# Norms by halves of a row on two engines, transposes between products, and the last rows split over two engines

## Chip, core and metric

The kernel runs on one core of a Trainium2 chip. The metric is the device time in microseconds of one execution; lower is better. All inputs start in HBM, and the output ends there. The engines are TensorE (PE), VectorE (DVE), ScalarE (ACT), GpSimd (POOL) and SyncE (SP), each with its own queue of instructions that runs in order; semaphores tie them together.

## What is computed

A decoder trunk of two layers over 256 rows of 1024 columns in float32: latent attention, a dense SwiGLU mixer, then sliding-window attention and a mixture of 8 experts with 2 chosen for each row, and a last norm. Before each part stands the same norm:

```python
def rmsnorm(x, g):
    xf = x.astype(jnp.float32)
    y = xf * lax.rsqrt(jnp.mean(xf * xf, axis=-1, keepdims=True) + EPS)
    return (y * g.astype(jnp.float32)).astype(x.dtype)
...
    for l in range(DEPTH):
        xn = rmsnorm(h, g_attn[l])
        if l < N_A_LAYERS:
            h = h + mla(xn, ...)
        else:
            if b == 0:
                k_band, v_band, pos_band = shared_band_kv(h, positions, kv_g, kv_w, kv_b)
            h = h + swa_sink(xn, ...)
        xn = rmsnorm(h, g_ffn[l])
        h = h + (swiglu(xn, ...) if l % 2 == 0 else moe(xn, ...))
    return rmsnorm(h, g_final)
```

## The kernel before

The residual rows stay in SBUF as `h`, two tiles of 128 rows (t = 0, 1) by 1024 columns. Everything is written out by hand: each engine has one program, and the order of the instructions in it is the order of the code.

The program runs through these stages: latent attention (to about 116 us), the dense mixer (to about 321 us), keys, values and queries of the second attention and that attention (to about 410 us), routing, then a loop over the experts (from about 425 to 1243 us), and the last norm. The mixer's products use weights split in a high and a low part: ScalarE casts (`w_hi_part`, L800), VectorE subtracts (`w_lo_part`, L1754), unit by unit; TensorE multiplies high by high and low (L1140, L1141) and low by high (L1144). A unit is half of the k range of one chunk of gate or up weights. Units 0 and 1 are run for t = 0 and then for t = 1 before the others start.

Weights come through one area, `ring`, by DMAs that SyncE issues. The dense ones (L620) wait until the weights that lie there have been used. The experts' pieces (896 KB, L658; the down weights in pairs, L661) wait in `room_for` until their place is free: for the first expert until the dense weights above it are used, the last of them by the product with `swo`; afterwards until TensorE has read a piece that lies there.

A norm of a row tile is a chain over four engines. ScalarE squares 1024 columns and sums them (`squares`, L746; L968 at the end). VectorE turns the sum into mean plus EPS (L1599), GpSimd raises it to the power -0.5 (L697), VectorE scales the row (L1606, or L1608 with the gain at the end). Then TensorE transposes the scaled row in eight blocks (`rows_to_T`, L982), and VectorE takes the blocks out of PSUM with the gain: `evac_xT` (L1621) in two halves of four blocks, or, before the dense mixer, `evac_xT_split`, which writes the gained halves (L1762), lets ScalarE cast them to `xT_hi` (L809) and subtracts to get `xT_lo` (L1767). `add_out` (L1746), `ffn_add` (L1823) and `add_rows` (L1990) add a product, 512 columns at a time, to `h`. At the end of the dense mixer the four additions are split by the first tile's norm: two before it, two behind it. There the scaled rows are transposed once and taken out twice, to `xT2` with the gain of keys and values and to `xT` with the gain of the attention. `L1243` makes keys, `L1247` and `L1248` values, `L1264` queries (`sq_products`).

GpSimd has little else in its queue: some small loads, the bias `swa_b_o` added to `h` (L725), two copies of prefetched pieces (L738), and the powers. The final gain `g_final` lies in `gfin`, a row repeated over the partitions, loaded long before it is used. At the end the two tiles are scaled by VectorE and stored by two DMAs that ScalarE issues (L973); SyncE waits for both.

## Time and profile before

| what | us |
|---|---|
| median of 3 runs | 1260.67 |
| lowest, highest | 1260.46, 1261.53 |
| the profiled execution | 1258.74 |
| its span, first to last instruction | 1256.1 |
| mean granted TensorE clock, share of full | 0.996 |

In the profiled execution TensorE is busy for 1203.2 us, VectorE for 315.7, ScalarE for 256.1 and GpSimd for 30.2. 413 MB are moved by DMA. Matmuls are pipelined and their busy time is modelled, so the rows that matter are those with an engine's idle time (in square brackets, with what ended it) and the DMA share of a stretch.

### The profile page before, as it was taken

How to read it: one execution, taken by the hardware profiler on the slowest of the kernel's cores; microseconds unless marked ns; L12 is line 12 of the kernel's file. 1: busy time of each engine (PE TensorE's matmuls, PEld its weight loads, DVE VectorE, ACT ScalarE, POOL GpSimd, SP SyncE). 2: the span in 40 equal slices, each digit the busy share in tenths (PEclk: the TensorE clock that was granted, in tenths of full speed). 3: DMA queues.
4: the chain of work that ended last, by engine and by line, in shares of the span. 5: the costliest groups of instructions: out<-in, count | busy, mean ns of one | idle time of the engine just before them, and what ended most of it. 6: DMA issues, size and time to landing. Idle time of an engine off the chain costs nothing.

```text
span 1256.1 us, 20334 instructions
## 1 busy us (share of the span) xinstructions
PE 1203.2 (96%) x8373; PEld 610.5 (49%) x8374; DVE 315.7 (25%) x716; ACT 256.1 (20%) x470; POOL 30.2 (2%) x48
## 2 busy tenths in 40 slices
PE   6999999999899999898999999999999999999997
PEld 4765777778665534333333433433343343334333
DVE  2355566667353400100010010010001101000102
ACT  2252433333154111011010101102101210211111
POOL 2100000000101100000000000000000000000000
PEclk9999999999999999999999999999999999999999
DMA  9612644326622699999999999999999999999994
GB/s 339 226 68 97 239 165 171 134 103 236 257 77 101 248 423 423 419 420 428 420 419 424 421 419 422 425 419 419 425 419 417 425 422 419 422 425 410 411 427 176
DMA packets 73021, 413.17 MB, mean 329 GB/s; under 512 B 6591, under 2 KB 11837, under 8 KB 64493
## 3 DMA queue, kind: packets, MB, share of 16 engines
q1 hardware_dynamic: 71708, 409.65, 80.5%
q8 instruction: 65, 1.06, 0.3%
q0 software_dynamic: 944, 1.29, 0.3%
q10 hardware_dynamic: 288, 1.05, 0.2%
q14 instruction: 16, 0.12, 0.0%
HBM read 410.91 MB, written 1.05 MB: 328 GB/s over the span
## 4 chain that ended last, share of the span: by engine, by line
PE 81%; DMA 9%; DVE 4%; issue 2%; ACT 2%; SPq 1%; POOL 0%; DVEq 0%; ACTq 0%; POOLq 0%
PE ps L1468 17%; PE ps L1448 11%; PE ps L1443 6%; PE ps L1426 6%; DMA ring<-in_moe_w_up 5%; PE ps L1535 4%; DMA ring<-in_moe_w_down 4%; PE ps L1144 4%; PE ps L1140 4%; PE ps L1141 4%; PE ps L1430 3%; PE ps L1499 3%; PE ps L1313 2%; PE ps L1106 2%; PE ps L1519 2%
## 5 line engine op out<-in xcount | busy, mean ns | idle before, releaser
L1468 PE MATMUL ps<-ring,arena 128*64 128x448 f32 x640 | 251.1, 545 | 9.2 <-issue 4.3
L1469 PE MATMUL ps<-ring,arena 128*64 128x448 f32 x640 | 251.2, 545 | 0.0
L1448 PE MATMUL ps<-ring,arena 128*32 128x448 f32 x1152 | 161.4, 539 | 0.0
L1468 PEld LDWEIGHTS ps<-ring,arena 128*64 128x64 f32 x640 | 84.5, 137 | 156.3 <-issue 142.4
L1449 PE MATMUL ps<-ring,arena 128*32 128x448 f32 x384 | 160.0, 539 | 0.0
L2007 DVE TENSOR_TENSOR arena<-arena,ps 64x448 f32<-64x448 f32 (+1 forms) x64 | 38.5, 613 | 369.2 <-ACT arena L910 190.7
L1535 PE MATMUL ps<-ring,arena 128*64 128x512 f32 x280 | 125.1, 596 | 5.0 <-DMA ring<-in_moe_w_down 5.0
L1536 PE MATMUL ps<-ring,arena 128*64 128x512 f32 x280 | 125.1, 596 | 0.0
L1443 PE MATMUL ps<-ring,arena 128*32 128x448 f32 x768 | 90.4, 542 | 5.8 <-DVE arena L2007 4.0
L1448 PEld LDWEIGHTS ps<-ring,arena 128*32 128x32 f32 x1152 | 48.0, 110 | 93.8 <-issue 93.8
L1754 DVE TENSOR_TENSOR w_lo<-ring,w_hi 128x2048 fp32r<-128x2048 f32 x33 | 75.5, 2292 | 60.3 <-ACT w_hi L800 59.2
L1426 PE MATMUL ps<-ring,arena 128*32 128x512 f32 x504 | 87.1, 593 | 0.0
L800 ACT CAST w_hi<-ring 128x2048 fp32r<-128x2048 f32 x33 | 62.9, 1908 | 114.2 <-PE ps L1144 114.2
L1427 PE MATMUL ps<-ring,arena 128*32 128x512 f32 x168 | 86.0, 593 | 0.0
L1469 PEld LDWEIGHTS ps<-ring,arena 128*64 128x64 f32 x640 | 84.5, 137 | 0.0
L1535 PEld LDWEIGHTS ps<-ring,arena 128*64 128x64 f32 x280 | 36.7, 137 | 78.9 <-issue 73.4
L1140 PE MATMUL ps<-w_hi,xT_hi 128*128 128x512 f32 (+1 forms) x192 | 71.6, 380 | 2.8 <-DVE xT_lo L1767 2.8
L1141 PE MATMUL ps<-w_hi,xT_lo 128*128 128x512 f32 (+1 forms) x192 | 70.1, 372 | 0.0
L921 ACT COPY arena<-ps 128x320 f32<-128x320 f32 (+3 forms) x48 | 21.8, 455 | 211.5 <-PE ps L1519 211.5
L1430 PE MATMUL ps<-ring,arena 128*32 128x256 f32 x672 | 51.6, 379 | 0.0
L1990 DVE TENSOR_TENSOR h<-h,ps 128x512 f32<-128x512 f32 x36 | 24.7, 687 | 104.4 <-PE ps L1499 104.4
L1443 PEld LDWEIGHTS ps<-ring,arena 128*32 128x32 f32 x768 | 22.4, 109 | 52.3 <-issue 43.2
(292 smaller groups left out, 1421.6 us busy)
## 6 DMA issues: line engine op xcount, KB each, us to landing
ring<-in_moe_w_down SPq DMA_DIRECT2D x64, 1792.0 KB, 21.1
ring<-in_moe_w_gate SPq DMA_DIRECT2D x127, 896.0 KB, 19.4
...
```

What stands on the lines that cost most here:

```text
L1140: pe.matmul(out, lhs[0][:, k, c], rhs_hi[:, k, :], start=(first and k == 0), stop=False)
L1141: pe.matmul(out, lhs[1][:, k, c], rhs_hi[:, k, :], start=False, stop=False)
L1426: pe.matmul(ps[32 * j:32 * j + 32, bank, :], thirds[j], left, start=first, stop=last)
L1427: pe.matmul(ps[SLOTS:P, bank, :], thirds[2], right, start=first, stop=last)
L1430: mm = pe.matmul(ps[q:q + 32, bank + 1, 0:LASTQ], thirds[j], right[:, cols:cols + LASTQ], start=first, stop=last)
L1443: pe.matmul(ps[q:q + 32, 4 + c // 2, 0:CH], thirds[j], wg[:, (c + e) * CH:(c + e + 1) * CH], start=first, stop=last)
L1448: pe.matmul(ps[32 * j:32 * j + 32, c, 0:CH], thirds[j], wu[:, c * CH:(c + 1) * CH], start=first, stop=last)
L1449: mm = pe.matmul(ps[SLOTS:P, c, 0:CH], thirds[2], wg[:, c * CH:(c + 1) * CH], start=first, stop=last)
L1468: pe.matmul(ps[0:NARROW, c, 0:CH], lhs, wu[:, cols], start=(k == 0), stop=(k == KD - 1))
L1469: mm = pe.matmul(ps[64:64 + NARROW, c, 0:CH], lhs, wg[:, cols], start=(k == 0), stop=(k == KD - 1))
L1535: pe.matmul(ps[0:NARROW, DOWN_BANK, :], lhs, w[:, 0:512], start=first, stop=last)
L1536: mm = pe.matmul(ps[64:64 + NARROW, DOWN_BANK + 1, :], lhs, w[:, 512:1024], start=first, stop=last)
```

## The change

Seven semaphores are added. The two early norms (n = 1 before the dense mixer, n = 2 behind it) and the last one are done in another way; the first norm of the program and the one before the experts stay.

Squares: ScalarE squares the two 512-wide halves of a tile in instructions of their own, each as soon as its addition is done, with the factor 1/32 inside, so that the sums add up to the mean (`square_half`). GpSimd adds EPS to the lower half's sum (`rstd_of_halves`), and ScalarE adds the upper half's sum to that by an Identity activation of one column (`mean_of_halves`), in place of VectorE's instruction. GpSimd's power stays. Scaling: VectorE scales the lower half (`scale_lower`), ScalarE the upper (`scale_upper`); TensorE waits for the upper only ahead of the fifth transposed block.

Order: before the dense mixer the transposes of t = 1 go between unit 0 and unit 1 of t = 0, and each unit of t = 1 waits for its own half of the transposed rows. Behind the mixer VectorE does three additions before the scaling, and takes out `xT2` of both tiles before `xT` of either; the transposes of t = 1 go between keys and values of t = 0, and the key products wait by halves.

End: the last additions signal `h_final`. Row tile 0 is scaled by VectorE as before and stored by SyncE. Of row tile 1, GpSimd multiplies the upper half by the gain, between row 0's power and row 1's EPS addition, and ScalarE scales it and stores it; VectorE does the lower half, SyncE stores it.

TensorE's order before, around the transposes of t = 1 ahead of the dense mixer. The two groups of four L1144 rows of t = 0 end unit 0 and unit 1; this is the second:

```order
L1144 MATMUL ps<-w_lo,xT_hi 128x512 x4
L982 MATMUL ps<-cst,xn 128x128 [waits xn_ready]
L982 MATMUL ps<-cst,xn 128x128 x7
L1140 MATMUL ps<-w_hi,xT_hi 128x512 [waits xT_ready]
L1141 MATMUL ps<-w_hi,xT_lo 128x512
```

and now, where the L1193 row (the former L1144) is the first of the two:

```order
L1193 MATMUL ps<-w_lo,xT_hi 128x512 x4
L1031 MATMUL ps<-cst,xn 128x128 [waits xn_ready]
L1031 MATMUL ps<-cst,xn 128x128 x3
L1031 MATMUL ps<-cst,xn 128x128 [waits xn_ready_a]
L1031 MATMUL ps<-cst,xn 128x128 x3
L1189 MATMUL ps<-w_hi,xT_hi 128x512
```

The eight transposes moved ahead by one unit, and have a second wait in their middle.

VectorE's order before, at the end of the dense mixer (L1823 `ffn_add`, L1621 `evac_xT`, twice for each tile):

```order
L1823 TENSOR_TENSOR h<-h,ps 128x512 [waits fh_added,fdown_mm] x2
L1599 TENSOR_SCALAR stat<-stat 128x1 [waits ssq_ready]
L1606 TENSOR_SCALAR xn<-h,stat 128x1024 [waits rstd_ready]
L1823 TENSOR_TENSOR h<-h,ps 128x512 [waits fh_added,fdown_mm] x2
L1621 TENSOR_TENSOR xT<-ps,vecT 128x4x128 [waits xT_mm]
L1621 TENSOR_TENSOR xT<-ps,vecT 128x4x128
L1621 TENSOR_TENSOR xT<-ps,vecT 128x4x128 [waits xT_mm]
L1621 TENSOR_TENSOR xT<-ps,vecT 128x4x128
L1599 TENSOR_SCALAR stat<-stat 128x1 [waits ssq_ready]
L1606 TENSOR_SCALAR xn<-h,stat 128x1024 [waits rstd_ready]
L1621 TENSOR_TENSOR xT<-ps,vecT 128x4x128 [waits xT_mm]
L1621 TENSOR_TENSOR xT<-ps,vecT 128x4x128
```

and now (L1882 `ffn_add`, L1668 `scale_lower`, L1680 `evac_xT`):

```order
L1882 TENSOR_TENSOR h<-h,ps 128x512 [waits fh_added,fdown_mm] x3
L1668 TENSOR_SCALAR xn<-h,stat 128x512 [waits rstd_ready]
L1882 TENSOR_TENSOR h<-h,ps 128x512 [waits fh_added,fdown_mm]
L1680 TENSOR_TENSOR xT<-ps,vecT 128x4x128 [waits xT_mm]
L1680 TENSOR_TENSOR xT<-ps,vecT 128x4x128
L1668 TENSOR_SCALAR xn<-h,stat 128x512 [waits rstd_ready]
L1680 TENSOR_TENSOR xT<-ps,vecT 128x4x128 [waits xT_mm]
L1680 TENSOR_TENSOR xT<-ps,vecT 128x4x128
L1680 TENSOR_TENSOR xT<-ps,vecT 128x4x128 [waits xT_mm]
L1680 TENSOR_TENSOR xT<-ps,vecT 128x4x128
L1680 TENSOR_TENSOR xT<-ps,vecT 128x4x128 [waits xT_mm]
L1680 TENSOR_TENSOR xT<-ps,vecT 128x4x128
```

The third addition stands ahead of the scaling, the second tile's scaling and its `xT2` ahead of the first tile's `xT`, and the mean is gone.

GpSimd's order at the end of the program, before (L733 loads the final gain, L738 copies a prefetched piece):

```order
L697 TENSOR_TENSOR stat<-stat,cst 128x1 [waits ms_ready] x2
L733 DMA xT<-in_g_final 128x1024 [waits swo_mm]
L738 COPY ring<-arena 128x1792 [waits gu_read,ahead_loaded]
L738 COPY ring<-arena 128x1792
L697 TENSOR_TENSOR stat<-stat,cst 128x1 [waits ms_ready] x2
```

and now (L758 the copy, L718 EPS, L709 power, L762 the gain):

```order
L758 COPY ring<-arena 128x1792 [waits gu_read,ahead_loaded]
L758 COPY ring<-arena 128x1792
L718 TENSOR_SCALAR stat<-stat 128x1 [waits half_squares]
L709 TENSOR_TENSOR stat<-stat,cst 128x1 [waits ms_ready]
L762 TENSOR_TENSOR xn<-h,xT 128x512 [waits h_final,rel_loaded]
L718 TENSOR_SCALAR stat<-stat 128x1 [waits half_squares]
L709 TENSOR_TENSOR stat<-stat,cst 128x1 [waits ms_ready]
```

The EPS addition and the power of tile 1 come behind a 512-wide product.

The diff, with the declarations of semaphores cut to those that the text names:

```diff
@@ -155,7 +155,14 @@
...
+        self.half_squares = sem("half_squares")
+        self.eps_added = sem("eps_added")
+        self.xn_ready_a = sem("xn_ready_a")
+        self.h_final = sem("h_final")
...
@@ -674,7 +681,12 @@
                     sp.nop()
-            sp.wait_ge(s.out_stored, 32)
+            rows = out[0].rearrange("(t p) d -> t p d", p=P)
+            sp.wait_ge(s.row_done, 1)
+            sp.dma_start(rows[0], xn[:, 0, :]).then_inc(s.out_stored, 16)
+            sp.wait_ge(s.row_done, 2)
+            sp.dma_start(rows[1][:, 0:512], xn[:, 1, 0:512]).then_inc(s.out_stored, 16)
+            sp.wait_ge(s.out_stored, 48)
@@ -700,6 +712,12 @@
+            def rstd_of_halves(n, t):
+                pool.wait_ge(s.half_squares, 4 * n + 2 * t + 1)
+                nc.gpsimd.tensor_scalar(stat[:, 10 + t:11 + t], stat[:, 6 + t:7 + t], EPS, None, ALU.add).then_inc(s.eps_added, 1)
+                rstd(4 + t, 2 + t)
             pool.wait_ge(s.consts_loaded, 16)
@@ -714,13 +732,15 @@
                 pool.dma_start(tabs_h[32 * kk + 1:32 * kk + 32, 1, c], rel_bias[0:31, :]).then_inc(s.rel_loaded, 16)
-            rstd_rows()
-            rstd_rows()
+            for n in range(2):
+                for t in range(TT):
+                    rstd_of_halves(n, t)
...
             pool.wait_ge(s.xn_ready, 6)
+            pool.wait_ge(s.xn_ready_a, 4)
             for t in range(TT):
@@ -736,7 +756,11 @@
                 nc.gpsimd.tensor_copy(piece(m), ahead[:, n, :]).then_inc(s.piece_landed[m % LAPS], 16)
-            rstd_rows()
+            rstd_of_halves(2, 0)
+            pool.wait_ge(s.rel_loaded, 16 * 10)
+            pool.wait_ge(s.h_final, 4)
+            nc.gpsimd.tensor_tensor(xn[:, 1, 512:D], h[:, 1, 512:D], gfin[:, 512:D], ALU.mult).then_inc(s.gained_last, 1)
+            rstd_of_halves(2, 1)
@@ -744,6 +768,23 @@
                 act.activation(xn[:, t, :], h[:, t, :], ACT.Square, accum_out=stat[:, t:t + 1]).then_inc(s.ssq_ready, 1)
+            def square_half(t, half, done, count, junk):
+                act.wait_ge(done, count)
+                act.activation(junk, h[:, t, half * 512:(half + 1) * 512], ACT.Square, scale=D ** -0.5,
+                               accum_out=stat[:, 6 + 2 * half + t:7 + 2 * half + t]).then_inc(s.half_squares, 1)
+            def mean_of_halves(n, t):
+                act.wait_ge(s.half_squares, 4 * n + 2 * t + 2)
+                act.wait_ge(s.eps_added, 2 * n + t + 1)
+                act.activation(stat[:, 2 + t:3 + t], stat[:, 8 + t:9 + t], ACT.Identity, bias=stat[:, 10 + t:11 + t]).then_inc(s.ms_ready, 1)
+            def scale_upper(n, t):
+                act.wait_ge(s.rstd_ready, 5 + 2 * n + t)
+                act.activation(xn[:, t, 512:D], h[:, t, 512:D], ACT.Copy, scale=stat[:, 4 + t:5 + t]).then_inc(s.xn_ready_a, 1)
@@ -802,8 +843,10 @@
             for t in range(TT):
-                act.wait_ge(s.h_attn0, 2 * t + 2)
-                squares(t)
+                for half in range(2):
+                    square_half(t, half, s.h_attn0, 2 * t + half + 1, xn[:, t, half * 512:(half + 1) * 512])
+                mean_of_halves(0, t)
+                scale_upper(0, t)
                 for b in range(2):
@@ -825,8 +868,10 @@
             for t in range(TT):
-                act.wait_ge(s.fh_added, 4 * FCH - 2 * (TT - 1 - t))
-                squares(t)
+                for half in range(2):
+                    square_half(t, half, s.fh_added, 4 * (FCH - 1) + 2 * t + half + 1, xn[:, t, half * 512:(half + 1) * 512])
+                mean_of_halves(1, t)
+                scale_upper(1, t)
             act.wait_ge(s.kT_mm, 2)
@@ -964,13 +1009,15 @@
             for t in range(TT):
-                act.wait_ge(s.h_added, items * 4 + (2 * t + 3))
-                act.activation(xT[:].rearrange("p k n -> p (k n)")[:, t * D:(t + 1) * D], h[:, t, :], ACT.Square,
-                               accum_out=stat[:, t:t + 1]).then_inc(s.ssq_ready, 1)
+                for half in range(2):
+                    square_half(t, half, s.h_final, 2 * t + half + 1, xT[:].rearrange("p k n -> p (k n)")[:, half * 512:(half + 1) * 512])
+                mean_of_halves(2, t)
             orow = out[0].rearrange("(t p) d -> t p d", p=P)
-            for t in range(TT):
-                act.wait_ge(s.xn_ready, 9 + t)
-                act.dma_start(orow[t], xn[:, t, :]).then_inc(s.out_stored, 16)
+            act.wait_ge(s.gained_last, 1)
+            act.wait_ge(s.rstd_ready, 12)
+            act.activation(xn[:, 1, 512:D], xn[:, 1, 512:D], ACT.Copy, scale=stat[:, 5:6]).then_inc(s.row_done_a, 1)
+            act.wait_ge(s.row_done_a, 1)
+            act.dma_start(orow[1][:, 512:D], xn[:, 1, 512:D]).then_inc(s.out_stored, 16)
@@ -979,6 +1026,8 @@
                 for k in range(KD):
+                    if k == 4 and n >= 1:
+                        pe.wait_ge(s.xn_ready_a, 2 * (n - 1) + t + 1)
                     mm = pe.transpose(ps[:, off + 2 * t + k // 4, (k % 4) * P:(k % 4 + 1) * P], xn[:, t, k * P:(k + 1) * P], ident)
@@ -1215,10 +1264,11 @@
             for t in range(TT):
-                if t == 1:
-                    rows_to_T(1, 1, 4)
-                    pe.wait_ge(s.xT_ready, 8)
                 for q in range(2):
+                    if (t, q) == (0, 1):
+                        rows_to_T(1, 1, 4)
+                    if t == 1:
+                        pe.wait_ge(s.xT_ready, 7 + q)
                     p_ = gu_passes(q, t)
@@ -1236,12 +1286,13 @@
             for t in range(TT):
-                if t == 1:
-                    rows_to_T(2, 1, 0)
-                pe.wait_ge(s.xT_ready, 10 + 4 * t)
                 for k in range(KD):
+                    if k % 4 == 0:
+                        pe.wait_ge(s.xT_ready, 9 + 2 * t + k // 4)
                     mm = pe.matmul(ps[:, 4, t * P:(t + 1) * P], w[:, k, 0:P], xT2[:, k, t * P:(t + 1) * P], start=(k == 0), stop=(k == KD - 1))
                 mm.then_inc(s.kT_mm, 1)
+                if t == 0:
+                    rows_to_T(2, 1, 0)
                 b = 7 if t == 0 else 5
@@ -1486,7 +1537,7 @@
-            def scatter(i, t):
+            def scatter(i, t, last=False):
@@ -1494,7 +1545,9 @@
                     j = 2 * t + half
-                    if t == 1:
+                    if t == 1 and last:
+                        pe.wait_ge(s.h_final, half + 1)
+                    elif t == 1:
                         pe.wait_ge(s.h_added, i * 4 + (half + 2))
@@ -1575,8 +1628,8 @@
                     pe_item(i, False)
-            scatter(items, 0)
-            scatter(items, 1)
+            scatter(items, 0, True)
+            scatter(items, 1, True)
@@ -1607,6 +1660,12 @@
                                              op0=ALU.mult, op1=ALU.mult).then_inc(s.xn_ready, 1)
+            def scale_lower(t):
+                norms[0] += 1
+                dve.wait_ge(s.rstd_ready, norms[0])
+                dve.tensor_scalar(xn[:, t, 0:512], h[:, t, 0:512], stat[:, 4 + t:5 + t], None, ALU.mult).then_inc(s.xn_ready, 1)
@@ -1771,11 +1830,11 @@
             add_out(1, s.wo_mm, s.h_attn0)
-            norm_rows(0)
+            scale_lower(0)
             add_out(2, s.wo_mm, s.h_attn0)
...
             add_out(3, s.wo_mm, s.h_attn0)
-            norm_rows(1)
+            scale_lower(1)
             evac_xT_split(1)
@@ -1843,13 +1902,13 @@
             ffn_add(n0 + 1)
-            norm_rows(0)
             ffn_add(n0 + 2)
+            scale_lower(0)
             ffn_add(n0 + 3)
             evac_xT(2, 0, 0, xT2, V_KVG)
+            scale_lower(1)
+            evac_xT(2, 1, 0, xT2, V_KVG)
             evac_xT(2, 0, 0, xT, V_GA1)
-            norm_rows(1)
-            evac_xT(2, 1, 0, xT2, V_KVG)
             evac_xT(2, 1, 0, xT, V_GA1)
@@ -1983,11 +2042,11 @@
-            def add_rows(i, j):
+            def add_rows(i, j, done=s.h_added):
                 t, half = j // 2, j % 2
...
                 hv = h[:, t, half * 512:(half + 1) * 512]
-                dve.tensor_tensor(hv, hv, ps[:, SCATTER_BANK[j], :], ALU.add).then_inc(s.h_added, 1)
+                dve.tensor_tensor(hv, hv, ps[:, SCATTER_BANK[j], :], ALU.add).then_inc(done, 1)
@@ -2022,11 +2081,14 @@
             for j in range(4):
-                add_rows(items, j)
+                add_rows(items, j, s.h_final)
             dve.wait_ge(s.rel_loaded, 16 * 10)
-            for t in range(TT):
-                norm_rows(t, gfin)
+            for t, c in ((0, slice(0, D)), (1, slice(0, 512))):
+                norms[0] += 1
+                dve.wait_ge(s.rstd_ready, norms[0])
+                dve.scalar_tensor_tensor(out=xn[:, t, c], in0=h[:, t, c], scalar=stat[:, 4 + t:5 + t], in1=gfin[:, c],
+                                         op0=ALU.mult, op1=ALU.mult).then_inc(s.row_done, 1)
...
 _INS = ["x", "positions", "mla_w_in", "mla_g_q", "mla_g_kv", "mla_w_uq", "mla_w_ukv", "mla_w_o", "kv_g", "kv_w", "kv_b",
```

## Rows read from the trace of the kernel before

**Rows 1.** The page: DMA busy share in 40 slices of the span, in tenths.

```profile
DMA  9612644326622699999999999999999999999994
```

**Rows 2.** Stretches: us, busy time of each engine, PEclk, DMA share, GB/s.

```profile
440.00:450.00 10.00, 10.00 (x56) 3.73 (x54) 0.49 (x3) 0.37 (x1) 0.00 (x0) 1.00 1.01 415
...
1230.00:1235.00 5.00, 5.00 (x28) 2.05 (x29) 0.00 (x0) 1.04 (x4) 0.00 (x0) 1.00 0.72 307
```

**Rows 3.** Timeline, first site: start us, us, engine, line, operation, out<-in [idle before].

```profile
117.03 1.06 ACT L746 ACTIVATE xn<-h 128x1024 f32<-128x1024 f32 x1 [5.65 <-DVE h L1746]
...
117.99 0.18 ACT L746 ACTIVATION_READ_ACCUMULATOR xn<-h 128x1 f32 x1
...
118.44 0.56 POOL L697 TENSOR_TENSOR stat<-stat,cst 128x1 f32<-128x1 f32 x1 [12.72 <-DVE stat L1599]
...
118.86 0.39 PE L1140 MATMUL ps<-w_hi,xT_hi 128*128 128x512 f32 x1
...
119.04 0.75 DVE L1606 TENSOR_SCALAR xn<-h,stat 128x1024 f32<-128x1024 f32 x1 [0.67 <-POOL stat L697]
...
121.59 1.04 PE L982 MATMUL ps<-cst,xn 128*128 128x128 f32 x8
...
122.66 1.29 DVE L1762 TENSOR_TENSOR arena<-ps,vecT 128x512 f32<-128x512 f32 x2 [2.87 <-PE ps L982]
...
123.38 1.22 ACT L809 CAST xT_hi<-arena 128x512 fp32r<-128x512 f32 x2 [5.21 <-DVE arena L1762]
...
124.10 1.29 DVE L1767 TENSOR_TENSOR xT_lo<-arena,xT_hi 128x512 fp32r<-128x512 f32 x2 [0.15 <-ACT xT_hi L809]
...
125.45 0.50 PE L1140 MATMUL ps<-w_hi,xT_hi 128*128 128x512 f32 x1 [2.83 <-DVE xT_lo L1767]
```

**Rows 4.** Timeline, second site, columns as in Rows 3.

```profile
318.83 1.06 ACT L746 ACTIVATE xn<-h 128x1024 f32<-128x1024 f32 x1 [8.60 <-DVE h L1823]
...
320.18 0.61 PE L1144 MATMUL ps<-w_lo,fhhT_hi 128*128 128x512 f32 x2
...
321.50 1.28 DVE L1823 TENSOR_TENSOR h<-h,ps 128x512 f32<-128x512 f32 x2
...
321.64 1.09 PE L982 MATMUL ps<-cst,xn 128*128 128x128 f32 x8 [0.85 <-DVE xn L1606]
...
324.21 2.02 PE L1243 MATMUL ps<-xT,ring 128*128 128x128 f32 x16 [1.47 <-DVE xT L1621]
...
330.84 2.05 PE L1243 MATMUL ps<-xT,ring 128*128 128x128 f32 x16 [1.38 <-DVE xT L1621]
...
335.02 14.03 PE L1264 MATMUL ps<-xT,ring 128*64 128x256 f32 x128
```

**Rows 5.** Timeline, last rows of the program, columns as in Rows 3.

```profile
1248.33 0.69 DVE L1990 TENSOR_TENSOR h<-h,ps 128x512 f32<-128x512 f32 x1 [0.17 <-PE ps L1499]
...
1249.05 1.06 ACT L968 ACTIVATE xT<-h 128x1024 f32<-128x1024 f32 x1 [0.76 <-DVE h L1990]
...
1249.77 1.28 DVE L1608 SCALAR_TENSOR_TENSOR xn<-h,stat,xT 128x1024 f32<-128x1024 f32 x1 [0.69 <-POOL stat L697]
...
1251.78 1.28 DVE L1608 SCALAR_TENSOR_TENSOR xn<-h,stat,xT 128x1024 f32<-128x1024 f32 x1 [0.66 <-POOL stat L697]
```

**Rows 6.** Tile out: time from the issue of a store to its landing.

```profile
DMA to landing us min/median/max: 2.6/2.8/3.0
```

**Rows 7.** Timeline elsewhere: GpSimd on wide tiles, and VectorE beside it.

```profile
343.77 4.67 POOL L725 TENSOR_TENSOR h<-h,xn 128x1024 f32<-128x1024 f32 x2 [7.78 <-DMA xn<-in_swa_b_o]
...
429.00 3.29 POOL L738 COPY ring<-arena 128x1792 f32<-128x1792 f32 x2 [11.54 <-PE ps L1469]
...
429.90 0.69 DVE L1990 TENSOR_TENSOR h<-h,ps 128x512 f32<-128x512 f32 x1 [2.92 <-PE ps L1499]
```

**Rows 8.** Timeline elsewhere: an Identity activation of ScalarE, and a table load.

```profile
332.93 0.47 ACT L831 ACTIVATE arena<-ps,vecT 128x256 f32<-128x256 f32 x1 [8.96 <-PE ps L1243]
...
349.96 1.28 ACT L845 ACT_TABLE_LOAD   x1
```

3 lines of the change are left out of this document (added).

## The prediction, made before the change was run

> **What bounds the kernel now.** I read the 40 slices first. The DMA digit is 9 in every slice from the fifteenth on until the last but one [rows 1], that is from about 440 us on. The table of stretches says the same more closely: the DMA engines are at 1.01 and 415 GB/s from 440 us, and they leave that level only around 1230 us [rows 2]. So the last two thirds of the kernel are one uninterrupted stream of expert weights. What happens inside that stretch matters little; what counts is when the stream can start, and what is left after it ends. It starts when the product with `swo` has freed the ring and when TensorE has read the first pieces of the ring (the waits on `swo_mm` and `gu_read` in `room_for`), and both come at the end of a chain that TensorE walks without a break through attention, dense mixer and second attention. DMA is far from full there [rows 1]. A microsecond of TensorE's idle time removed before 410 us should therefore bring the whole stream, and the end, forward by a microsecond.
>
> Next I looked for idle time of TensorE beside norms, which are what the change touches. There are three places.
>
> First site, the norm between MLA and dense mixer. The second row's transposes stand behind both t = 0 products and run at 121.59; then TensorE stands for 2.83 us until VectorE, ScalarE and VectorE again have made the high and low parts of the transposed rows [rows 3]. The rows themselves were scaled by 119.04 + 0.75 = 119.79 us, so the transposes wait for their place in the order, not for data.
>
> Second site, after the dense mixer. TensorE's last down product ends at 320.18 + 0.61 = 320.79. It then stands 0.85 us for the scaled rows, 1.47 us for the first transposed tile and 1.38 us for the second [rows 4]: 3.70 us in the 14.23 us between 320.79 and 335.02, hence 10.53 us of work. Part of that is VectorE's own order: the two additions that start at 321.50 were due at about 319.5 and 320.8, but stood behind the wait for the norm, and the evacuation stands behind them.
>
> Third site, the last norm. The fourth addition ends at 1248.33 + 0.69 = 1249.02. The second row's chain then is: square over 1024 columns at 1249.05, mean on VectorE (behind the 1.28 us of the first row), power on GpSimd, scaling 1251.78 to 1253.06 [rows 5], store. Nothing else is left to run; its length counts in full.
>
> **First site after the change.** Addition 3 of `add_out` still ends at 117.0. By then the lower half's square has been done, so that only the upper half is left: half of 1.06, 0.53 us, and the read of the accumulator, 0.18 [rows 3], give 117.74. The mean is now one ScalarE instruction on one column. No row shows that size; the smallest piece of an activation that stands here is the 0.18 us of the accumulator read, and a 256-wide Identity took 0.47 [rows 8]. I take 0.2 and a handover of 0.05: 118.0. GpSimd's power takes 0.56 with about 0.1 for handovers [rows 3]: 118.65. Half the scaling is between half of 0.75 and 0.75, I take 0.45 on VectorE; on ScalarE a 512-wide pass is 1.22 / 2 = 0.61 [rows 3], which the transposes need only for their fifth tile. TensorE is ready at 118.86 (the row where the second unit starts [rows 3]) and can transpose from 119.15: a new wait of 0.3 us. GpSimd's added addition of EPS uses the lower half's sum and is long done. Queued behind the waiting transposes is unit 1 of t = 0. Transposes to 120.20, unit 1 (118.86 to 121.59, 2.73 us) to 122.95. Meanwhile VectorE starts the gains at 120.25 and needs, as before, 124.10 - 122.66 + 1.29 / 2 = 2.09 us to the first low half (122.34) and 2.73 us to the second (122.98, needed only at about 125.7). The t = 1 products start at 122.95 instead of 125.45: **2.5 us** earlier. Bounds: 2.8 if the scaled rows come at 118.86, about 1.9 if each new small instruction costs 0.3 more. The casts and subtractions of the dense mixer start from TensorE's progress and move with it.
>
> **Second site.** Addition 3 of 4 now runs at 319.46, before the scaling. The upper half's square starts at 318.83 as before, ends with its read at 319.54, mean 319.79, power 320.4, lower scaling 320.85, upper 321.0. Transposes start at 320.87 instead of 321.64 and take 1.09, to 321.96. The fourth addition has gone into that time. The finer wait lets the product start after one of the two evacuations, half of 1.3 plus a handover of 0.15: 322.8 instead of 324.21. The eight k products take about 1.88 (324.7), the second transposes 1.09 (325.8); their rows are ready at about 323.95, since ScalarE begins the half squares of t = 1 when it has scaled its upper half. Then come the v products of t = 0, 2.3 us, and under these VectorE does `xT2` of t = 1 (325.85 to 327.15), so nothing is left of the 1.38. Idle time is 0.1 + 0.85 instead of 3.70, and `sq_products` start at 332.2 instead of 335.02: **2.8 us**. The `xT` evacuations that are moved behind end at about 329.7, before their use at 332.2. Bounds: 2.0 (small instructions 0.3 dearer on both chains) and 3.0.
>
> **Third site.** The upper half of row 1 gets its gain on GpSimd: after addition 4 at 1249.1, and behind it in GpSimd's queue stand the EPS addition and the power of row 1, which ScalarE and then everybody wait for. A 1024-wide product of two tiles took 4.67 / 2 = 2.33 us there [rows 7], so 512 wide is 1.17, to 1250.3. EPS addition 0.56 as the power (no row shows it; bounds 0.2 and 0.75): 1250.85. Mean 0.25, to 1251.1; power with handovers 0.65, to 1251.75. That is just when the power was ready before, at 1251.78. The scaling is now 0.64 (half of 1.28) on VectorE beside 0.61 on ScalarE: 1252.4 instead of 1253.06, so **0.6 us** gained. The store of row 1 is the same 512 KB in two issues from two queues; a store took 2.6 to 3.0 us to land [rows 6], I count no difference, with 0.4 either way as bounds. Row 0's store moves to SyncE's queue, which is empty then.
>
> The price of GpSimd's 1.17 us hangs on who else reads. Here row 0's scaling by VectorE, 1.28 us long with two operands from the same memory, starts at 1249.0, at the same moment. The nearest row has GpSimd copying from 429.00 and VectorE adding at 429.90 in its usual 0.69 [rows 7], so side by side without loss, but with one operand of VectorE from PSUM. I take no loss. The other bound is that GpSimd stands for the whole 1.28.
>
> The Trainium skill has a rule for this, "SBUF — State Buffer", section "SBUF: two separate sides": a VectorE instruction with two SBUF inputs and a GpSimd instruction that reads SBUF exclude each other for the whole instruction, whoever starts first. No row here shows such a pair. By that rule the third site would lose instead of gain, as in the first rival.
>
> **Sum.** 2.5 + 2.8 + 0.6 = 5.9 us. Against the profiled execution, 1258.74 us (span 1256.1 and 2.6 around it), that is 1252.8. The median of the runs is 1260.67, 1.9 us above the profiled one, so the prediction for the median is 1260.67 - 5.9 = **1254.8 us**.
>
> **Rivals.** (a) *GpSimd stands behind VectorE at the end.* Gained half from 1250.35 to 1251.5, EPS 1252.1, mean 1252.4, power 1253.05, scaling 1253.7: 0.65 later than now. Total 2.5 + 2.8 - 0.65 = 4.65: 1256.0. For it: the two instructions start within 0.1 us of each other; against: only the one-operand row. Chance 0.33.
> (b) *One of the early gains is hidden.* For instance the dense mixer is held by its casts and subtractions rather than by TensorE, and takes the first site's 2.5 back: 3.4 left, 1257.3. Against it: TensorE is the engine that the others wait for in this stretch, and VectorE's and ScalarE's queues are moved by the same amount. Chance 0.10.
> (c) *The other side, slower.* ScalarE's Identity lies in another function table than Square and Copy. A load of a table costs 1.28 us [rows 8], and each mean would pay one before and one behind. At the first site the transposes wait 2.6 us more (gain gone), at the second 2.6 on the first row and as much again on the second, of which 0.7 hides, so 4.4 lost against 2.8 gained; at the end four changes, of which some 4 us show. Total +5: 1265.7. It decides from about 6 us of visible table loads. Against it: an Identity at 332.93, behind a Square, started with no load ahead of it [rows 8]. Chance 0.03.
> (d) *The split doesn't do what it says*: the small instructions cost so much that the split chains end no sooner than whole ones. The two moves of the transposes and of the additions still pay at both early sites, about 1.9 + 1.8, and the end loses 0.7: 1257.7. Chance 0.09.
>
> **How the numbers follow.** The forecast has 0.42 and its own range is 1253.6 to 1255.8. With rival (a) that makes 0.75; to hold 8 in 10 the range has to take in a part of (d) and (b) and the lower bounds of the sum (3.0 + 2.8 + 1.0 gives 1253.9, and the profiled execution ran 1.9 below the median): 1253.0 to 1257.7. A measurement of this kernel tells about 0.2%, 2.5 us, from no change, that is below 1258.2 is faster: forecast, (a), (d) and the better part of (b), 0.89. Within 0.2%: 0.08. Slower: 0.03.
>
> **What would show it.** In the profile after: TensorE's idle time before the t = 1 products of the first units gone and a wait of about 0.3 us before the moved transposes; `sq_products` 5.3 us earlier than 335.02; the DMA share at 1.01 some 5.3 us earlier, with the stretch from there to the last weight piece unchanged in length. If that stretch is longer instead, the premise that the stream only shifts is wrong. At the end, GpSimd's 512-wide product should start at the end of the fourth addition and take 1.2 us; if it starts or ends 1.2 us later, it is (a). A table load around a mean shows (c).

## The result and the profile after

| | before | after |
|---|---|---|
| median, us | 1260.57 (4 runs, 1260.10 to 1261.53) | 1253.16 (4 runs, 1252.29 to 1255.29) |
| the profiled execution | 1258.74 | 1255.29 |
| its span | 1256.1 | 1253.1 |

The ratio of the times, taken over all runs, is 0.9945, with a 95% interval from 0.9932 to 0.9958: 6.9 us faster, give or take 1.6. The two medians alone are 7.41 us apart. Gains below are taken from such ratios. The prediction was 1254.8 (1253.0 to 1257.7), faster; the measured median lies 0.16 us inside the fast end of that range. The two profiled executions differ by less, 3.45 us: the one of before was faster than all four runs of its median, the one of after the slowest of its four. In the one of after the latent attention reached the dense mixer 1.25 us later (116.95 for 115.70) than in the one of before, ahead of anything that the change touches. So lengths between two events are compared here, not their clock times. The first products of the mixer, before and then after:

```profile
115.70 0.80 PE L1140 MATMUL ps<-w_hi,xT_hi 128*128 128x512 f32 x1
```

```profile
116.95 0.79 PE L1189 MATMUL ps<-w_hi,xT_hi 128*128 128x512 f32 x1
```

The page of after: the DMA digits are 9 from the same fifteenth slice on as in [rows 1], and the fourteenth is 7 instead of 6.

```profile
PE   6999999999999999898999999999999999999996
...
PEclk9999999999999999999999999999999999999998
DMA  9612754436631799999999999999999999999994
```

**First site**, timeline of after; columns as in [rows 3], of which these are the counterparts:

```profile
118.27 0.63 ACT L775 ACTIVATE xn<-h 128x512 f32<-128x512 f32 x1 [5.02 <-DVE h L1805]
118.81 0.19 ACT L775 ACTIVATION_READ_ACCUMULATOR xn<-h 128x1 f32 x1
119.03 0.30 ACT L782 ACTIVATE stat<-stat 128x1 f32<-128x1 f32 x1
119.41 0.58 POOL L709 TENSOR_TENSOR stat<-stat,cst 128x1 f32<-128x1 f32 x1 [5.85 <-ACT stat L782]
120.02 0.72 ACT L787 ACTIVATE xn<-h,stat 128x512 f32<-128x512 f32 x1 [0.70 <-POOL stat L709]
120.02 0.48 DVE L1668 TENSOR_SCALAR xn<-h,stat 128x512 f32<-128x512 f32 x1 [1.78 <-POOL stat L709]
120.56 1.09 PE L1031 MATMUL ps<-cst,xn 128*128 128x128 f32 x8 [0.29 <-DVE xn L1668]
121.41 0.48 PE L1189 MATMUL ps<-w_hi,xT_hi 128*128 128x512 f32 x1
...
124.25 0.39 PE L1189 MATMUL ps<-w_hi,xT_hi 128*128 128x512 f32 x1
```

The bracket on the transposes (L1031) is the new wait, 0.29 us. The t = 1 products start at 124.25 with no bracket: the 2.83 us that stood there [rows 3] are gone. The unit-0 products of t = 0 began at 116.95, so the way from there is 7.30 us; before it was 9.75.

**Second site**, timeline of after, against [rows 4]:

```profile
318.65 0.61 PE L1193 MATMUL ps<-w_lo,fhhT_hi 128*128 128x512 f32 x2
319.44 0.68 DVE L1882 TENSOR_TENSOR h<-h,ps 128x512 f32<-128x512 f32 x1
319.58 1.09 PE L1031 MATMUL ps<-cst,xn 128*128 128x128 f32 x8 [0.32 <-DVE xn L1668]
321.55 2.02 PE L1292 MATMUL ps<-xT,ring 128*128 128x128 f32 x16 [0.88 <-DVE xT L1680]
323.40 1.04 PE L1031 MATMUL ps<-cst,xn 128*128 128x128 f32 x8
324.28 1.95 PE L1298 MATMUL ps<-ring,xT 128*128 128x128 f32 x16
326.57 2.05 PE L1292 MATMUL ps<-xT,ring 128*128 128x128 f32 x16
330.75 0.44 PE L1315 MATMUL ps<-xT,ring 128*64 128x256 f32 x2
```

The idle time of TensorE is 0.32 + 0.88 instead of 0.85 + 1.47 + 1.38. From the end of the last down product (319.26) to the query products (330.75) it takes 11.49 us instead of 14.23.

**End**, timeline of after, against [rows 5]:

```profile
1244.80 0.69 DVE L2049 TENSOR_TENSOR h<-h,ps 128x512 f32<-128x512 f32 x1 [0.17 <-PE ps L1552]
1245.44 1.28 DVE L2090 SCALAR_TENSOR_TENSOR xn<-h,stat,xT 128x1024 f32<-128x1024 f32 x1
1245.64 2.21 POOL L762 TENSOR_TENSOR xn<-h,xT 128x512 f32<-128x512 f32 x1 [0.31 <-DVE h L2049]
1247.93 0.22 POOL L718 TENSOR_SCALAR stat<-stat 128x1 f32<-128x1 f32 x1
1248.25 0.29 ACT L782 ACTIVATE stat<-stat 128x1 f32<-128x1 f32 x1 [2.00 <-POOL stat L718]
1248.62 0.57 POOL L709 TENSOR_TENSOR stat<-stat,cst 128x1 f32<-128x1 f32 x1 [0.47 <-ACT stat L782]
1249.23 0.75 DVE L2090 SCALAR_TENSOR_TENSOR xn<-h,stat,xT 128x512 f32<-128x512 f32 x1 [2.50 <-POOL stat L709]
1249.29 0.72 ACT L1018 ACTIVATE xn<-xn,stat 128x512 f32<-128x512 f32 x1 [0.74 <-POOL stat L709]
```

GpSimd's product stands as 2.21 us, not 1.17. The last scaling ends 4.52 us behind the fourth addition; before it was 4.04 (1249.02 to 1253.06 [rows 5]). The end lost 0.48 us.

**The expert stream**, first piece behind `swo` and first piece of the second round (issues on SyncE's queue), before and then after:

```profile
412.03 0.33 SPq L658 DMA_DIRECT2D ring<-in_moe_w_gate  x1
...
433.92 0.33 SPq L658 DMA_DIRECT2D ring<-in_moe_w_gate  x1
```

```profile
407.76 0.33 SPq L665 DMA_DIRECT2D ring<-in_moe_w_gate  x1
...
430.20 0.33 SPq L665 DMA_DIRECT2D ring<-in_moe_w_gate  x1
```

To compare kernels I took six lengths from each profiled execution. All are differences of two start or end times in the timelines. `swo` stands for the product with it, a scatter for the product that adds the experts' rows back, a piece for the DMA of an expert's weights:

| us | first mixer product to t = 1 products | to the end of the down products | to the query products | query products to the first piece behind `swo` | second round of pieces to the last scatter | 4th addition to last scaling |
|---|---|---|---|---|---|---|
| before | 9.75 | 205.09 | 14.23 | 77.01 | 810.5 | 4.04 |
| after | 7.30 | 202.31 | 11.49 | 77.01 | 810.7 | 4.52 |
| e1_first_site | 7.31 | 202.26 | 14.23 | 77.0 | 811.1 | 4.04 |
| e2_second_site | 9.75 | 206.67 | 11.50 | 77.0 | 811.0 | 4.03 |
| e3_end_alone | 9.75 | 206.58 | 14.23 | 77.0 | 810.3 | 4.51 |
| e4_order_alone | 7.83 | 203.14 | 13.72 | 77.0 | 810.7 | 4.03 |
| e6_gpsimd_first | 7.31 | 202.29 | 11.50 | 77.0 | 810.3 | 4.03 |
| e7_product_earlier | 7.31 | 202.25 | 11.50 | 77.0 | 810.3 | 2.90 |
| e8_both_early | 7.31 | 202.35 | 11.50 | 77.0 | 811.0 | 4.04 |
| e10_filled_second | 9.75 | 206.59 | 14.22 | 77.0 | 810.3 | 4.04 |

The second column runs from the same first product as the first and contains it. Two readings set the questions for the experiments. The three changed lengths add up to 2.78 + 2.74 - 0.48 = 5.04 us, against a measured 6.9 (give or take 1.6): perhaps something beyond the path was gained. And the second column holds 205.1 or 206.6 for kernels whose mixer is the same.

### The profile page after: what moved, and what is told of

Read it like the earlier page. It is cut to its first block, busy times and chain, and to the rows that moved or that the text cites. A ratio compares the mean times of both kernels' runs of the same rounds, so it can differ in the third digit from the quotient of the medians.

```text
span 1253.1 us, 20363 instructions
## 1 busy us (share of the span) xinstructions
PE 1205.7 (96%) x8373; PEld 612.8 (49%) x8374; DVE 313.5 (25%) x710; ACT 262.8 (21%) x493; POOL 33.9 (3%) x55
## 3 DMA queue, kind: packets, MB, share of 16 engines
HBM read 410.91 MB, written 1.05 MB: 329 GB/s over the span
## 4 chain that ended last, share of the span: by engine, by line
PE 80%; DMA 11%; DVE 3%; issue 2%; ACT 2%; POOL 0%; SPq 0%; DVEq 0%; ACTq 0%; POOLq 0%
PE ps L1519 17%; PE ps L1499 11%; DMA ring<-in_moe_w_up 7%; PE ps L1494 6%; PE ps L1477 6%; DMA ring<-in_moe_w_down 4%; PE ps L1193 4%; PE ps L1189 4%; PE ps L1190 4%; PE ps L1481 3%; PE ps L1588 3%; PE ps L1552 3%; PE ps L1364 2%; PE ps L1155 2%; PE ps L1572 2%
```

## The experiments

My theory after the result: each early site gives what the path shows (about 2.5 and 2.8), the end loses about 0.5 because GpSimd's product and VectorE's scaling exclude each other; and the rest, if it is one, comes from TensorE's clock, which the removed waits no longer let fall. The clock was not yet in it when e1 to e4 were expected; it came from their profiles. The rivals: that the order of the transposes alone did it and the halves nothing, that the end gained after all, and that the rest is scatter between runs.

### One site at a time, and both early ones

e1_first_site has only the first site's change, e2_second_site only the second's, e8_both_early both, with the old end. The core of e1 against before:

```diff
-                act.wait_ge(s.h_attn0, 2 * t + 2)
-                squares(t)
+                for half in range(2):
+                    square_half(t, half, s.h_attn0, 2 * t + half + 1, xn[:, t, half * 512:(half + 1) * 512])
+                mean_of_halves(0, t)
+                scale_upper(0, t)
...
-                if t == 1:
-                    rows_to_T(1, 1, 4)
-                    pe.wait_ge(s.xT_ready, 8)
                 for q in range(2):
+                    if (t, q) == (0, 1):
+                        rows_to_T(1, 1, 4)
+                    if t == 1:
+                        pe.wait_ge(s.xT_ready, 7 + q)
...
-            norm_rows(0)
+            scale_lower(0)
```

> The kernel before with the change at the first site alone (halves and moved transposes ahead of the dense mixer). My theory, that idle time of TensorE ahead of the expert stream is worth itself: the t = 1 products start 2.5 us sooner relative to the first product of the mixer, the stretch from there to the end is as long as before, total -2.5 us. Rival, the casts and subtractions of the mixer take it back: the products start sooner, but the last down product of the mixer does not, total 0.

Measured: 1255.98, ratio 0.9964 (0.9953 to 0.9975), so 4.5 us faster. The path gives 2.44 to the t = 1 products, and 2.83 by the end of the mixer (205.09 to 202.26). Of the further 0.39, 0.17 lies in the first unit of t = 1, where the way from the first product to the L1144 rows (L1180 in e1) takes 1.98 us behind the wait and 1.81 without it; the rest was not located. The time fell further than the 2.5 us expected; the section on the clock gives the likely reason.

For e2, the edits of the second site alone (halves, order of the additions and evacuations, `rows_to_T(2, 1, 0)` between keys and values):

```diff
-                if t == 1:
-                    rows_to_T(2, 1, 0)
-                pe.wait_ge(s.xT_ready, 10 + 4 * t)
                 for k in range(KD):
+                    if k % 4 == 0:
+                        pe.wait_ge(s.xT_ready, 9 + 2 * t + k // 4)
...
+                if t == 0:
+                    rows_to_T(2, 1, 0)
...
-            norm_rows(0)
             ffn_add(n0 + 2)
+            scale_lower(0)
```

> The kernel before with the change at the second site alone (behind the dense mixer). Theory: 2.8 us less between the last down product and the query products, total -2.8 us. Rival, the stream of experts is fed by something that does not move: the query products come sooner, the first piece of the stream or its end does not, total 0 to -1.

Measured: 1257.16, ratio 0.9979 (0.9967 to 0.9991), 2.6 us; on the path 14.23 to 11.50, 2.73. As expected.

> The change at both early sites, and the end as in the kernel before. The profiles of the parts say: 2.5 us at the first site, 2.7 at the second, the stretch from the query products to the last scatter product as before; the end 4.04 us from the last addition to the last scaling instead of 4.5. So -5.2 us by the path, and if the clock fall behind the first site's wait goes too, -6.2 to -6.7; 0.5 us better than the whole change. Rival: the whole change gains more than this, since the end helps after all.

Measured: 1253.58, ratio 0.9949 (0.9937 to 0.9961), 6.4 us. The two sites add up, and the gain is above the path's 5.5 (2.74 + 2.73) by 0.9 us, where e1's is above its path by 1.7; the intervals are 1.5 us wide to either side and hold both.

### The end alone

e3_end_alone has both early sites as before, and only the last norm changed:

```diff
-                add_rows(items, j)
+                add_rows(items, j, s.h_final)
...
+            nc.gpsimd.tensor_tensor(xn[:, 1, 512:D], h[:, 1, 512:D], gfin[:, 512:D], ALU.mult).then_inc(s.gained_last, 1)
...
-            for t in range(TT):
-                norm_rows(t, gfin)
+            for t, c in ((0, slice(0, D)), (1, slice(0, 512))):
+                norms[0] += 1
+                dve.wait_ge(s.rstd_ready, norms[0])
+                dve.scalar_tensor_tensor(out=xn[:, t, c], in0=h[:, t, c], scalar=stat[:, 4 + t:5 + t], in1=gfin[:, c],
+                                         op0=ALU.mult, op1=ALU.mult).then_inc(s.row_done, 1)
```

> The kernel before with the change at the end alone (tile 1 split over two engines, GpSimd's product in between). If GpSimd's 512-wide product stands behind VectorE's 1.28 us of tile 0, as the profile of the changed kernel suggests with 2.21 us for it where 1.17 was expected: +0.4 to +0.5 us, that is the same within the measurement. If my forecast for the end was right after all: -0.6 us.

Measured: 1259.69, ratio 1.0 (0.9988 to 1.0011). The interval, 1.5 us to either side, holds the 0.47 us that the path shows lost. It is the path, not the timing, that rules out a gain at the end.

### Order against halves

e4_order_alone moves the transposes, the additions and the finer waits at both early sites, but squares, sums and scales whole tiles as before:

```diff
             ffn_add(n0 + 1)
-            norm_rows(0)
             ffn_add(n0 + 2)
+            norm_rows(0)
             ffn_add(n0 + 3)
             evac_xT(2, 0, 0, xT2, V_KVG)
-            evac_xT(2, 0, 0, xT, V_GA1)
             norm_rows(1)
             evac_xT(2, 1, 0, xT2, V_KVG)
+            evac_xT(2, 0, 0, xT, V_GA1)
```

> The kernel before with the orders of both early sites moved (transposes, the third addition, evacuations, waits by halves of the transposed tile), but squares, mean and scaling of whole tiles as before, and the end as before. Theory: the moves are most of it. At the first site the scaled tile comes 1.0 us after TensorE is ready, gain 1.8 us; at the second 1.7 us; total -3.5 us against -5.2 with the halves. Rival, the halves are what matters: total -1 or less. Rival, the moves are all: -5.

Measured: 1255.34, ratio 0.9959 (0.9945 to 0.9972), 5.2 us. At the first site the path shortens by 1.92 of the whole change's 2.44; the new wait ahead of the transposes is 0.82 us instead of 0.29. At the second its profile has a stretch at the lower clock:

```profile
320.00:322.00 2.00, 1.13 (x11) 0.92 (x10) 1.41 (x3) 1.15 (x2) 0.00 (x0) 1.00 0.86 301
322.00:326.00 4.00, 4.00 (x24) 4.00 (x23) 0.94 (x3) 0.00 (x0) 0.55 (x1) 0.57 1.01 416
```

(stretches of e4, columns as in [rows 2]). The clock fell behind two waits of TensorE of 0.90 and 0.87 us. The key products there took 3.35 us instead of 2.02 [rows 4] and the transposes 1.39 instead of 1.04, so 1.6 to 1.7 us of the site's gain went into that: 0.51 by the table, about 2.1 without it, an estimate. The order alone thus carries some 4.0 of the 2.44 + 2.73 = 5.2 us of path, the halves the other 1.2; of this 0.52 is read at the first site (7.83 and 7.31), the rest hangs on the estimate. The median alone would fit the rival that the moves are all (-5) as well. With 1.1 to 1.5 us for the clock at the first site (below), 4.0 makes 5.1 to 5.5, and 5.2 was measured.

### GpSimd and VectorE at the end

e6_gpsimd_first is the changed kernel with one wait more: VectorE scales row 0 only when GpSimd's product is done.

```diff
             dve.wait_ge(s.rel_loaded, 16 * 10)
+            dve.wait_ge(s.gained_last, 1)
             for t, c in ((0, slice(0, D)), (1, slice(0, 512))):
```

> The changed kernel with one more wait: VectorE's scaling of row tile 0 at the end waits until GpSimd has done its 512-wide product. Theory (the two block each other, GpSimd came second): GpSimd's product takes 1.2 us instead of 2.2, its EPS addition comes 1.0 sooner, VectorE's tile 0 ends 1.3 later at about 2.6 us behind the last addition, and the last scaling ends about 3.6 us behind it instead of 4.5: 0.9 us faster than the changed kernel, by an added wait. Rival (the product simply costs 2.2 us): the product takes 2.2 us again, tile 0 ends 1.3 later, and the last scaling ends no sooner: 0 to +0.5.

```profile
1244.03 1.26 POOL L763 TENSOR_TENSOR xn<-h,xT 128x512 f32<-128x512 f32 x1 [0.31 <-DVE h L2050]
...
1245.40 1.28 DVE L2092 SCALAR_TENSOR_TENSOR xn<-h,stat,xT 128x1024 f32<-128x1024 f32 x1 [1.51 <-POOL xn L763]
...
1246.07 1.04 POOL L709 TENSOR_TENSOR stat<-stat,cst 128x1 f32<-128x1 f32 x1 [0.47 <-ACT stat L783]
```

(timeline of e6). The same product, with nothing beside it, takes 1.26 us instead of 2.21. Nothing but the order of the two was changed, so it was VectorE's scaling that held GpSimd. But the delay moved on: now the power of row 1, one column wide, starts while VectorE's two-operand scaling runs (to 1246.68), and takes 1.04 us instead of 0.57. The last scaling ends 4.03 behind the fourth addition, not the 3.6 that I expected: the 0.48 is regained and no more. Of that, 0.39 goes into the stores: from the last scaling to the end of the span it is 3.48 us in e6 and 3.09 in after, with 3.1 and 2.7 us from issue to landing for ScalarE's store. Median 1254.0, ratio 0.9946 (0.9933 to 0.9959), not to be told from the changed kernel.

e7_product_earlier (and e12_earlier_again, the same kernel) gives GpSimd the upper half of row 0, ready two additions earlier, and VectorE multiplies the upper half of row 1 in the wait for the power; both rows are then scaled by halves on two engines and stored in four parts.

```diff
-            pool.wait_ge(s.h_final, 4)
-            nc.gpsimd.tensor_tensor(xn[:, 1, 512:D], h[:, 1, 512:D], gfin[:, 512:D], ALU.mult).then_inc(s.gained_last, 1)
+            pool.wait_ge(s.h_final, 2)
+            nc.gpsimd.tensor_tensor(xn[:, 0, 512:D], h[:, 0, 512:D], gfin[:, 512:D], ALU.mult).then_inc(s.gained_first, 1)
...
-            for t, c in ((0, slice(0, D)), (1, slice(0, 512))):
+            for t, c in ((0, slice(0, 512)), (1, slice(0, 512))):
                 norms[0] += 1
+                if t == 1:
+                    dve.wait_ge(s.h_final, 4)
+                    dve.tensor_tensor(xn[:, 1, 512:D], h[:, 1, 512:D], gfin[:, 512:D], ALU.mult).then_inc(s.gained_last, 1)
```

> The changed kernel with another division of the end: GpSimd multiplies the upper half of row tile 0, not 1, by the gain, as soon as its addition is there, beside VectorE's additions (one operand in PSUM). VectorE scales the lower half of tile 0 (0.75 us), multiplies the upper half of tile 1 (0.65) and scales its lower half; ScalarE scales both upper halves; four stores. Theory: GpSimd's product takes 1.2 us there, nothing stands between addition 4 and the EPS addition of tile 1, and the last scaling ends 2.8 us behind the last addition instead of 4.5: 1.7 us faster than the changed kernel. If the product costs 2.2 us wherever it is: 3.5 to 3.8 us behind it.

```profile
1242.70 1.27 POOL L767 TENSOR_TENSOR xn<-h,xT 128x512 f32<-128x512 f32 x1
1242.77 0.69 DVE L2056 TENSOR_TENSOR h<-h,ps 128x512 f32<-128x512 f32 x1 [0.36 <-PE ps L1559]
...
1244.60 0.22 POOL L721 TENSOR_SCALAR stat<-stat 128x1 f32<-128x1 f32 x1
1244.63 0.75 DVE L2100 SCALAR_TENSOR_TENSOR xn<-h,stat,xT 128x512 f32<-128x512 f32 x1 [0.31 <-POOL stat L712]
...
1245.30 0.68 DVE L2098 TENSOR_TENSOR xn<-h,xT 128x512 f32<-128x512 f32 x1
...
1245.48 0.93 POOL L712 TENSOR_TENSOR stat<-stat,cst 128x1 f32<-128x1 f32 x1 [0.66 <-ACT stat L788]
```

(timeline of e7). The first two and the last two of these rows are both cases. Beside an addition that takes one operand from PSUM, GpSimd's product takes 1.27 us, as alone in e6, and the addition its usual 0.69; beside a product of two SBUF operands, the power takes 0.93 instead of 0.57. The middle two are the other way round: GpSimd's EPS addition starts 0.03 us ahead of a two-operand scaling, and neither is longer than elsewhere (0.22 and 0.75). So no run here shows GpSimd holding VectorE up. Median 1253.03, ratio 0.9943 (0.9931 to 0.9956); the last scaling ends 2.90 behind the fourth addition, against 4.52.

One more pair of runs set both beside each other:

> The changed kernel, unaltered, beside the others. The parts measured so far sum to -2.5 (first site), -2.7 (second), +0.5 (end) by the path, -4.7 us, and 1 to 1.5 us more if the kernel before mostly pays for a clock fall that this one cannot have: -5.7 to -6.2, ratio 0.9951 to 0.9955.

> The version with GpSimd's product on row tile 0 once more, beside the changed kernel on the same chip. Its profile showed 1.6 us less between the last addition and the last scaling and 0.3 us more behind it, so it should be 1.3 us faster than the changed kernel, -7.0 to -7.5 us against the kernel before. Rival: the stores eat the rest, and the two are equal.

Measured: e11 (the changed kernel) 1253.42, ratio 0.9948 (0.9934 to 0.9962); e12 1252.04, ratio 0.9938 (0.9924 to 0.9953). e12 is the fastest version that I ran, by 1.4 us over the changed kernel on the same chip. On the path it is 1.6 shorter, and some 0.3 of that go back into a later landing of the stores. The intervals of the two ratios overlap, and e7, the same kernel as e12, had 0.9943 against 0.9945 for the first measurement of the changed kernel. So that this version is faster stands on the path; the timing doesn't tell the two apart.

### The clock behind the first site's wait

TensorE stands for 2.83 us there in the kernel before [rows 3]. Stretches of before, e3, the filled kernel e10 (below) and after, all of them 126 to 128 us; PEclk, the seventh of the columns behind the stretch, is the granted clock:

```profile
126.00:128.00 2.00, 2.00 (x10) 1.61 (x9) 0.00 (x0) 0.00 (x0) 0.00 (x0) 1.00 1.03 410
```

```profile
126.00:128.00 2.00, 2.00 (x6) 1.56 (x5) 0.00 (x0) 0.00 (x0) 0.00 (x0) 0.50 1.03 413
```

```profile
126.00:128.00 2.00, 1.92 (x5) 1.53 (x6) 0.62 (x4) 0.00 (x0) 0.00 (x0) 0.50 1.01 406
128.00:130.00 2.00, 2.00 (x7) 1.58 (x6) 0.00 (x0) 0.00 (x0) 0.00 (x0) 0.66 1.03 399
```

```profile
126.00:128.00 2.00, 2.00 (x10) 1.65 (x10) 0.00 (x0) 0.78 (x1) 0.00 (x0) 1.00 1.01 406
```

0.50 is 1.2 GHz of 2.4. In e3 the stretch has 6 products where before has 10, and the products behind the wait run like this (timeline of e3):

```profile
125.32 0.79 PE L1181 MATMUL ps<-w_hi,xT_hi 128*128 128x512 f32 x1 [2.83 <-DVE xT_lo L1816]
125.91 0.63 PE L1182 MATMUL ps<-w_hi,xT_lo 128*128 128x512 f32 x1
...
128.46 0.39 PE L1182 MATMUL ps<-w_hi,xT_lo 128*128 128x512 f32 x1
```

0.63 us each instead of 0.39, for 3 us, which makes the mixer 1.5 us longer: 206.6 instead of 205.1 in the table. The clock was already down when the first product behind the wait started. Four kernels were profiled with the wait in place, one profile each: e2, e3 and e10 fell, before didn't. Ten profiles without the wait, shortened (after, e1, e4, e6, e7, e8, e11, e12) or filled with products (e5, e9), show 1.00 in that stretch. So among the kernels with the wait the profile that I predicted from is the exception. That the kernel before itself pays the 1.5 us in most executions is inferred from the three others. Its mean granted clock leans the same way without counting falls: 0.9956 over 74 executions of before, e2 and e3, 0.9965 over 49 of the eight kernels with the wait shortened.

To see that by itself I filled the wait. e5_filled_wait and e9_filled_again are the kernel before with three products that nobody reads; e10_filled_second has the same three in the waits of the second site, as a control that leaves the first one empty:

```diff
                     rows_to_T(1, 1, 4)
+                    for _ in range(3):
+                        pe.matmul(ps[:, 3, :], ident, cst[:, 0:512], start=True, stop=True)
                     pe.wait_ge(s.xT_ready, 8)
```

> The kernel before, and nothing of the change: only three 512-wide matmuls into a free bank, whose result nobody reads, are put where TensorE waits 2.8 us at the first site. Nothing of the path gets shorter: the t = 1 products start 9.75 us after the first product of the mixer as before. Theory A, formed from the first four runs: in the kernel before, the granted clock falls to half behind that wait in most executions (0.50 from 126 to 128 us in two of the three profiles that still have the wait), and this costs 1.5 us each time; with the wait filled the clock stays at 1.00 from 124 to 134 us, and the median falls by 0.5 to 1.5 us. Theory B: the fall has nothing to do with the wait; it is there again, and the median stays within 0.3 us.

> The run with the first site's wait filled, once more, to be compared with the next one, which has as many matmuls. Its last run was 6 us slower than the kernel before, by a pause of 5.3 us of TensorE ahead of the first expert product (1.0 us before), outside the place that I changed. Expected: the same pause again, the clock at 1.00 from 124 to 134 us again, 1266 to 1267 us.

> The kernel before with the same three extra matmuls, but in the waits of the second site (0.85, 1.47 and 1.38 us long) and none at the first. Theory A (the clock falls behind the unfilled wait of 2.8 us in most executions, 1.5 us each time) says 0.5 to 1.5 us slower than the run filled at the first site, and a granted clock of about 0.5 from 126 to 128 us if the profile hits such an execution. Theory B (no such cost): the two are equal within 0.3 us. On the pause ahead of the expert loop: if it comes from the length of TensorE's program ahead of the loop, it is 5.3 us here too; if it comes from the matmuls at the first site, it is 1.0 us and the time is 1260.

Measured: e5 1266.62, ratio 1.0049 (1.0036 to 1.0062); e9 1266.18, 1.0053 (1.0038 to 1.0067); e10 1267.73, 1.0066 (1.0052 to 1.008). All three are 6 to 8 us slower than before, where e5 had been expected a little faster. So as a timing the test failed. The cause lies elsewhere, ahead of the first expert product; timelines of before and of e5:

```profile
423.73 0.83 PE L1417 MATMUL ps<-arena,xn 128*128 128x96 f32 x6
425.58 0.59 PE L1468 MATMUL ps<-ring,arena 128*64 128x448 f32 x1 [1.02 <-issue]
```

```profile
432.22 1.00 PE L1470 MATMUL ps<-ring,arena 128*64 128x448 f32 x1 [5.29 <-issue]
433.01 0.95 PE L1470 MATMUL ps<-ring,arena 128*64 128x448 f32 x1
```

TensorE stands for 5.29 us (5.1 in e9, 6.58 in e10) in place of 1.02, waiting for nothing that the profile shows, and comes back at half the clock, 0.95 instead of 0.54 us for one product. From the first piece behind `swo` to the second round of pieces it is 29.7, 29.9 and 29.1 us in e5, e9 and e10, and 21.9 in before. The control shows that the pause comes wherever the three products stand; that it comes from the mere length of TensorE's program ahead of the expert loop is the likely reading, and not tested. On the clock itself the profiles still speak. The mixer took 205.1 us in e5 and e9 with the clock at 1.00, and 206.59 in e10 with 0.50 in the rows above. The timing doesn't decide: e10's median is 1.55 above e9's, but e10's profiled execution is 0.65 shorter than e9's, since 1.44 more in the mixer meets 0.85 less up to the second round of pieces and 0.88 less from there to the last scatter (810.27 for 811.15). The size of 1.5 us is shown in three profiles. The link to the wait rests on a count, three of four with it against none of ten without; how often the fall comes in unprofiled executions of before is not shown.

## Why the prediction was right, and where it wasn't

**What bounds the kernel** held. In all profiles the way from the query products to the first piece behind `swo` is 77.0 us, and the way from the second round of pieces to the last scatter 810.3 to 811.2: the expert stream only shifts. Between those two it is 21.89 us in before and 22.44 in after, 0.55 more by a stretch at the lower clock (last section). By clock time the second round comes 3.7 us sooner (433.92 to 430.20), not the 5.3 of the prediction's sign: 5.5 gained, less the later start of 1.25 and this 0.55. Rival (b), an early gain that is hidden, is out, since e1, e2 and e8 gave their gains and added up.

**First site**: 2.5 predicted, 2.45 in the profile of after. The wait ahead of the moved transposes was put at 0.3 and is 0.29 in the bracket. From start to start, as the prediction counted, the transposes come 0.45 us later than the second unit would have, and the unit behind them follows after 0.85 instead of 1.05. The pieces differ without moving the sum: mean 0.30 for 0.2, half scaling on VectorE 0.48 for 0.45, on ScalarE 0.72 for 0.61.

**Second site**: 2.8 predicted, 2.74 found, with 0.32 + 0.88 of idle time for 0.1 + 0.85. That the sum holds is partly luck: 0.25 us more idle time than predicted meets 0.24 less work (10.29 us where the prediction kept 10.53). The evacuations that were moved behind cost nothing, as said.

**End**: the step that failed is "I take no loss" for GpSimd's product beside VectorE's scaling. The term was +0.6 and is -0.48. The product took 2.21 us, for 1.17 assumed and 1.26 measured alone; the row that the 1.17 was worked out from, L725 [rows 7], is an addition, not a product as the prediction calls it. Rival (a) had the mechanism and put the loss at 0.65; mainly the EPS addition, 0.22 us for 0.56, made it smaller. The stores were counted as no difference, and from the last scaling to the end of the span it is 3.04 us in before and 3.09 in after. The row that I leaned on [rows 7] was true and of another kind: VectorE had one operand in PSUM there, and e7 shows that such a pair indeed runs side by side. The rule of the Trainium skill that the prediction quoted ("SBUF — State Buffer", section "SBUF: two separate sides") agrees with the pairs in which VectorE was first: after's product ends 1.13 us behind VectorE's scaling, the powers of e6 and e7 0.43 us behind VectorE's instruction, and the pair with a PSUM operand costs nothing. In the one pair where GpSimd was first (its EPS addition, 0.03 us ahead, in e7) neither engine lost anything, so that direction is not shown. When a rule names exactly the pair that a change makes, and the nearest row is of a different pair, the rule deserves more than 0.33.

**Sum**: 5.9 predicted, 6.9 measured (5.3 to 8.5 by the interval), 6.6 in e11. The path gives 5.04. The clock fall at the first site, in 3 of 4 profiles with the wait and in none of after's two, adds an estimated 1.1 (3/4 of 1.5) to 1.5: 6.1 to 6.5. So two misses nearly cancelled: the end was taken 1.1 us too well, and 1.1 to 1.5 us of clock were not foreseen at all. That the median falls into the range is luck in part: 1253.16 and e11's 1253.42 lie outside the 1253.6 to 1255.8 that the forecast gave as its own, and inside the wider range only because its fast end was set for other reasons, the small bounds of the sum and a fast execution. The same two terms fit the other runs: e1 2.8 + 1.1 to 1.5 against 4.5, e2 2.7 against 2.6, e8 5.5 + 1.1 to 1.5 against 6.4. What is left is within the intervals, which are as wide as the clock's term itself; the timings agree with it and don't prove it.

**Base**: the 1.9 us by which the median of before lay above its profile was carried over as it stood. Part of it is probably explained now, since that profile had no fall at the first site, and a fall costs 1.5.

Rival (c), table loads around the Identity, is out, and so is what it supposed, that Identity lies in another function table than Square and Copy: in after the Identity took 0.29 to 0.30 us directly behind the accumulator's read of a Square, and a Copy followed it, with no load. Rival (d), that the split doesn't pay, is out at the first site by 0.52 us; by the estimate above, halves carry 1.2 us beyond the order at both.
